# An encoder block on 8 cores: key order, bf16 gate weights, earlier constants, and five moved pieces of work

## The chip, the cores and the metric

The kernel runs on all 8 cores of one Trainium2 chip. Each core runs the same program on its own half of one batch element's sequence (4 batches, 2 halves); there is no traffic between cores. The metric is the device time of the slowest core in microseconds (us). On a core, TensorE (PE in the tables) multiplies, VectorE (DVE), ScalarE (ACT) and GpSimd (POOL) work on its results, and SyncE (SP) does nothing but issue transfers and wait. Each engine takes its instructions in the order in which they were written.

## The reference

The block is one layer of a bidirectional encoder, with D_MODEL 2048, 4096 positions, 6 differential heads of 128 (values 256 wide), a Fourier branch 512 wide and a feed-forward width of 5632.

```python
h = rmsnorm(x, g_mix); z = h @ w_in            # q | k | v | fourier | gate_a | gate_f
q = partial_rope(q, cos, sin); k = partial_rope(k, cos, sin)
p = softmax(q k^T / sqrt(128))                 # two maps per head
o = (p[0] - lam * p[1]) @ v
o = rmsnorm(o, g_subln) * (1 - LAMBDA_INIT)
branch_a = o @ w_attn_branch
branch_f = real(fft2(f, axes=(positions, channels), norm="ortho")) @ w_four_branch
x = x + (sigmoid(gate_a) * branch_a + sigmoid(gate_f) * branch_f) @ w_out
h2 = rmsnorm(x, g_ffn)
x = x + (silu(h2 @ w_gate) * (h2 @ w_up)) @ w_down
out = rmsnorm(x, g_final)
```

## The kernel before, in words

Everything is written through a small recording layer. `mm`, `act`, `tt`, `ts`, `stt`, `cp` and `dma` append one instruction to one engine's list, and the layer adds the waits between engines from the tiles that an instruction reads and writes. Nothing is reordered: what is written first on an engine stands first in its queue. Activations are kept transposed (features on the 128 partitions, 512 tokens wide), so that products are `128x512` matmuls. SP issues nearly all loads and stores; POOL issues the weight loads, which convert float32 in HBM to bf16 on the way.

**Projection, passes 0 to 3 (0 to 1147 us).** A pass P holds 1024 tokens. Its work is a list `plan` of units `('u', P, m)`, each a pair m of 128-wide column blocks of `w_in`, done with seven products in place of eight (a Strassen-like form: `prod`, with sums of weights from `combine_b` on DVE), and one entry `('f', P, None)` for the Fourier columns. Passes 0 and 1 are the core's own tokens and do all columns (gates only in pass 0; the other half of the gates is done inside the attention); passes 2 and 3 are the other half's tokens, and need only keys and values: 12 units each, in the orders `o2_m` and `o3_m` over `oth_m`. There `oth_m[0:6]` are the value pairs, `oth_m[6:9]` key pairs without rotation, and `oth_m[9:12]` key pairs that get rotary embedding (`rope`, six more DVE and three more ACT instructions a unit). While a pass runs, `form_gen` prepares the next pass's tokens in small steps between the products: loads of xT, squares on ACT with sums on DVE, then, in the last third, scaling and the operand sums on DVE. PE has 8 banks of PSUM for this, a unit uses 4. Results leave through 4 output buffers (`outb`) and SP. In pass 3 SP also loads the tables and data of the Fourier stage (`d_pre`, `d_load_tab`, `d_load_f`).

**Fourier stage (1147 to 1227 us).** 8 groups `gi` of 32 matmuls `ps<-d_t,d_f`, combined on DVE and ACT into `d_x`, and finished by `d_out(gi)`, which writes `yT_scr`. Constants of the attention (ones, lambda, the gains) are made at the head of this stage.

**Attention (1227 to 2281 us).** 24 steps `si` = (head h, query block qb of 512), each of 32 steps G (`r = G % 32`). A step G is: two score matmuls of 128 queries with 1024 keys (`rec_S`), one ACT exponential over `128x1024` (`rec_exp`), and beside them some value matmuls of the step si-1 (`pv_gen`) and some gate matmuls (`gate_gen`). A query tile `it` of 128 takes 8 steps G: 4 for the first map (into `p1b[it % 3]`), 4 for the second (into `p2b[it % 2]`). After that, `later` runs `combine_p` (DVE: scale both maps, add) and `turn` (SP: a transposing DMA of half a tile into `aT`). The keys of head h, map c, lie in `kT[(2*h + c) % 3]` and are loaded by `c_load_k`, the values by `c_load_v` (transposing DMAs too). `epilogue` does the head norm: `e1` is a ones matmul in one of two banks `pg`, which it shares with the gates, `e2` is on ACT, `e3` on DVE. The gates take 32 weight tiles (`gw_issue`), which are the columns that pass 0 had already loaded and converted once.

**Output projection and feed-forward (2281 to 4502 us).** The branches are joined, multiplied with `w_o`, and the sums of squares for the norm are reduced over partitions by a ones matmul (`make_R`) and turned into scales on ACT (`fin_R`), in `Rb`. Then come two halves `hf` of 1024 tokens: 44 gate/up blocks, then 16 blocks `dc` of the down projection, each for two token blocks j of 512. At the end 32 DVE instructions scale the output tiles and SP stores them.

## Time and profile before

| | |
|---|---|
| median of 3 runs | 4502.16 us (4494.06 to 4900.55) |
| the profiled execution | 4503.35 us, its slowest core (core 3) 4501.8 us from first to last instruction |
| cores | 4474.6 to 4501.8 us, granted TensorE clock 0.973 to 0.974 |
| PE, DVE, ACT busy | 4161.6 us (92%), 2600.3 us (58%), 1474.9 us (33%) |
| POOL busy | 270.8 us (6%) |
| DMA | 658.66 MB, 146 GB/s on average |

The busy share of PE is what is near its limit. A profiled execution lies 1.55 us above its own slowest core's span and 1.2 us above the median, so times below are changes to 4503.35. A row of a timeline reads: start, duration, engine, line and operation, the tile written, the tiles read, the shape, how many in a row, and in brackets the idle time just before with what ended it. `PEclk` is the granted share of TensorE's clock, DMA share the mean busy share of the 16 DMA engines.

### The profile page before, as it was taken

The numbers are of one execution on the slowest core, as the hardware profiler recorded it, in microseconds if no ns is written. First come the engines' busy times: TensorE is split into PE (matmuls) and PEld (weight loads), VectorE is DVE, ScalarE is ACT, GpSimd is POOL, SyncE is SP. The second block draws the span as 40 slices with busy tenths as digits, with TensorE's granted clock in tenths as the row PEclk, the third lists the DMA queues.
The fourth block names the chain that finished last, engine by engine and source line by source line (L and its number), as shares of the span: only waits on it lengthen the run. The fifth ranks groups of instructions, "written<-read, shape, count | busy, mean of one in ns | idle before, by whom it ended". The sixth has DMA issues, their size and how long they took to land.

```text
span 4501.8 us, 57298 instructions; the slowest of 8 cores (4474.6 to 4501.8 us)
## 1 busy us (share of the span) xinstructions
PE 4161.6 (92%) x18808; PEld 1844.2 (41%) x18808; DVE 2600.3 (58%) x3940; ACT 1474.9 (33%) x2583; POOL 270.8 (6%) x516
## 2 busy tenths in 40 slices
PE   6898999988898899879889997999999999999997
PEld 2443443433343334333334443444444444444443
DVE  6586667665266666656646445666642257776112
ACT  2322232312288888868821121111110011111000
POOL 0000000000000000000000000000000000000000
PEclk9999999999999999989999998999999999999998
DMA  6875686847598899998975697555557766665454
GB/s 161 200 157 124 129 190 134 185 102 179 139 186 152 164 171 168 167 150 151 167 196 156 170 236 201 85 86 91 87 114 160 158 128 132 127 134 93 92 103 128
DMA packets 678754, 658.66 MB, mean 146 GB/s; under 512 B 474944, under 2 KB 515904, under 8 KB 676416
## 3 DMA queue, kind: packets, MB, share of 16 engines
q0 software_dynamic: 73728, 264.27, 35.8%
q1 hardware_dynamic: 604736, 390.72, 35.4%
q8 instruction: 158, 2.59, 0.2%
q14 instruction: 132, 1.08, 0.1%
HBM read 692.61 MB, written 113.25 MB: 179 GB/s over the span
## 4 chain that ended last, share of the span: by engine, by line
PE 72%; DVE 8%; DMA 7%; SPq 5%; issue 4%; ACT 3%; DVEq 0%; ACTq 0%
PE ps L279 72%; SPq L954 3%; SPq L314 2%; DMA b_h<-xT 2%; ACT c_p L290 2%; DVE b_t L293 1%; DMA c_a<-c_p 1%; DVE c_p L297 1%; DVE b_h L302 1%; DMA c_k<-k_scr 1%; SPq L905 1%; DMA x_scr<-te 1%; DVE b_c L293 1%; ACT b_t L290 1%; DVE c_p L293 1%
## 5 line engine op out<-in xcount | busy, mean ns | idle before, releaser
L290 ACT ACTIVATE c_p<-ps 128x1024 bf16<-128x1024 f32 x768 | 783.1, 1022 | 193.6 <-PE ps L279 129.5
L279 PE MATMUL ps<-f_h,wc 128*128 128x512 bf16 x3520 | 775.1, 379 | 0.0
L279 PE MATMUL ps<-g_a,wr 128*128 128x512 bf16 x2816 | 608.1, 379 | 0.0
L279 PE MATMUL ps<-b_h,b_c 128*128 128x512 bf16 x2272 | 524.2, 388 | 87.7 <-ACT b_t L290 67.2
L279 PE MATMUL ps<-c_k,c_q 128*128 128x512 bf16 x1536 | 471.4, 389 | 84.8 <-ACT c_p L290 53.8
L279 PEld LDWEIGHTS ps<-f_h,wc 128*128 128x128 bf16 x3520 | 344.6, 98 | 416.5 <-issue 2.2
L279 PE MATMUL ps<-c_a,c_v 128*128 128x512 bf16 x1536 | 456.8, 389 | 5.1 <-DMA c_a<-c_p 4.5
L279 PEld LDWEIGHTS ps<-g_a,wr 128*128 128x128 bf16 x2816 | 275.6, 98 | 332.2
L293 DVE TENSOR_TENSOR gr<-ps,gr 128x512 f32<-128x512 f32 x352 | 242.3, 689 | 278.6 <-PE ps L279 278.5
L279 PEld LDWEIGHTS ps<-b_h,b_c 128*128 128x128 bf16 x2272 | 223.0, 100 | 380.6 <-issue 134.3
L279 PE MATMUL ps<-c_h,c_w 128*128 128x512 bf16 x1024 | 344.9, 388 | 35.4 <-DVE c_z L308 21.6
L279 PE MATMUL ps<-f_h,wr 128*128 128x512 bf16 x1408 | 320.6, 381 | 6.3 <-DVE f_h L293 6.2
L293 DVE TENSOR_TENSOR b_t<-ps,b_t 128x512 f32<-128x512 f32 x247 | 168.7, 687 | 216.8 <-PE ps L279 106.1
L297 DVE TENSOR_SCALAR c_p<-c_p,c_r 128x2048 bf16<-128x2048 bf16 x384 | 271.1, 748 | 11.2 <-DVE c_r L297 1.4
L279 PEld LDWEIGHTS ps<-c_k,c_q 128*128 128x128 bf16 x1536 | 145.1, 99 | 290.0 <-issue 152.6
L279 PE MATMUL ps<-b_h,b_w 128*128 128x512 bf16 x1136 | 256.8, 379 | 0.0
L293 DVE TENSOR_TENSOR c_p<-c_p,c_p 128x2048 bf16<-128x2048 bf16 x192 | 235.2, 1225 | 20.3 <-DVE c_p L297 0.5
L279 PEld LDWEIGHTS ps<-c_a,c_v 128*128 128x128 bf16 x1536 | 153.4, 100 | 200.7 <-issue 32.2
L279 PE MATMUL ps<-e_m,wr 128*128 128x512 bf16 x1024 | 221.3, 379 | 0.0
L279 PEld LDWEIGHTS ps<-f_h,wr 128*128 128x128 bf16 x1408 | 138.2, 98 | 175.1 <-issue 10.9
L290 ACT ACTIVATE b_t<-ps 128x512 f32<-128x512 f32 (+1 forms) x107 | 63.5, 594 | 400.1 <-PE ps L279 316.6
L279 PE MATMUL ps<-e_on,wr 128*128 128x512 bf16 x768 | 177.9, 382 | 10.6 <-DMA e_on<-oT_scr 5.9
(119 smaller groups left out, 3850.8 us busy)
## 6 DMA issues: line engine op xcount, KB each, us to landing
wr<-w_gu POOLq DMA_DIRECT2D x176, 512.0 KB, 6.9
b_w<-w_z POOLq DMA_DIRECT2D x144, 512.0 KB, 9.2
b_h<-xT SPq DMA_DIRECT2D x64, 512.0 KB, 15.9
wr<-w_dn POOLq DMA_DIRECT2D x64, 512.0 KB, 5.9
tm<-x_scr SPq DMA_DIRECT2D x96, 256.0 KB, 4.9
c_w<-w_z POOLq DMA_DIRECT2D x32, 512.0 KB, 7.6
z_scr<-c_z SPq DMA_DIRECT2D x64, 256.0 KB, 3.4
ez<-z_scr SPq DMA_DIRECT2D x32, 512.0 KB, 7.8
```

The source lines that it names most:

```text
L279: S.op('pe', lambda e: e.matmul(o, lhsT=l, rhs=r, start=st, stop=sp, skip_group_check=cont), reads, writes)
L290: S.op('act', lambda e: e.activation(out=o, in_=i, func=func, scale=scale, **kw), reads, writes)
L293: S.op(eng, lambda e: e.tensor_tensor(out=o, in0=a, in1=b, op=op), reads, writes)
L297: S.op(eng, lambda e: e.tensor_scalar(out=o, in0=a, scalar1=s1, scalar2=None, op0=op0), reads, writes)
L302: S.op(eng, lambda e: e.scalar_tensor_tensor(out=o, in0=a, scalar=s, in1=b, op0=op0, op1=op1), reads, writes)
L314: S.dma(q, lambda e: e.dma_start(out=o, in_=i), reads, writes, sem)
L905: S.dma('sp', lambda e: e.dma_start_transpose(out=vb[:, 8 * j:8 * j + 8, :], in_=vT_scr[2 * h:2 * h + 2, :, j * 1024:(j + 1) * 1024].rearr ...
L954: S.dma('sp', lambda e, A=A, P1=P1, sl=sl, hf=hf, qt=qt: e.dma_start_transpose(out=A[:, 16 * hf:16 * hf + 16, qt * 128:(qt + 1) * 128], in ...
```

## The change

Eight edits: (1) the order `o2_m` of pass 2; (2) in pass 0, each gate unit's converted weights are stored to a new scratch tensor `wb_scr` by SP, and `gw_issue` later loads from there; (3) the attention's constants are made at the program's start; (4) the Fourier tables are loaded in pieces of four k blocks, two pieces a unit from the third unit of pass 3, and all before the stage but the last table; (5) in the attention, `gmap` gives another order of query tiles and maps in the first half of a head's first query block and in the second half of its last, and key and value loads are moved; (6) the head norm's `e1` takes the bank that no gate matmul is using, when the gate's k stands between 5 and 10, and does not advance the rotation of the two banks; (7) `make_R` and `fin_R` of token blocks 2 and 3 move from ahead of the feed-forward to its third block; the last Fourier group's `d_out` moves into the attention; (8) the last two blocks dc of the down projection run by token block, and 12 of the 32 output tiles are scaled and stored beside the last product.

```diff
+            if P == 0 and m[0] >= 36:
+                gp = (m[0] - 36) // 2
+                dma('sp', wb_scr[gp], cur[0][:].rearrange("p (u a) k n -> p u (a k) n", u=2), [cur[1]], [d_wb[gp]], f'fo0_{gp}')
...
-                dma('pool', wg[i % 3][:], w_z[36 + i], [], [t_wg[i % 3]], f'wr{i % 3}')
+                dma('pool', wg[i % 3][:], wb_scr[i // 2, :, i % 2], [d_wb[i // 2]], [t_wg[i % 3]], f'wr{i % 3}')
...
-        o2_m = oth_m[0:6] + oth_m[7:12] + oth_m[6:7]
+        o2_m = oth_m[7:8] + oth_m[9:12] + oth_m[0:6] + oth_m[8:9] + oth_m[6:7]
...
+        def gmap(G):
+            si, r = G // 32, G % 32
+            b, ch = r // 4, r % 4
+            qt, c = b // 2, b % 2
+            if (si % 4 == 0 and r < 16) or (si % 4 == 3 and r >= 16):
+                qt, c = (b // 4) * 2 + b % 2, (b // 2) % 2
+            return si, r, qt, c, ch
...
             def e1():
-                st['p'] = pgget()[0:2]
+                if gst['k'] is not None and not 5 <= gst['k'] <= 10:
+                    later(1, e1)
+                    return
+                j_ = pgi[0] % 2
+                flush_pg(j_)
+                st['p'] = (pg[j_], t_pg[j_])
                 PB, tpb = st['p']
+                later(2, e2)
+                later(5, e3)
...
-            later(7, e1)
-            later(9, e2)
-            later(12, e3)
+            later(5, e1)
...
-        c_load_k(1, 0)
-        for j in range(4):
-            c_load_v(0, j)
...
+            if G == 2:
+                d_out(7, bk[4:6], t_bk[4:6], 'dve')
...
+            if G in (13, 18, 21, 26):
+                c_load_v(0, (13, 18, 21, 26).index(G))
             if r == 1:
-                if qb == 1 and 0 < h and h + 1 < NH:
+                if qb == 1 and h + 1 < NH:
                     c_load_k(h + 1, 0)
...
-            if qb == 3 and r == 27 and h + 1 < NH:
+            if qb == 3 and r == 23 and h + 1 < NH:
                 c_load_k(h + 1, 1)
...
-    for q in range(2, 4):
-        pb = bank()
-        make_R(q, pb)
-        fin_R(q, pb)
...
+            if hf == 0 and ff == 2:
+                for q in range(2, 4):
+                    pb = bank()
+                    make_R(q, pb)
+                    fin_R(q, pb)
...
+            dn_out(14, 0, dn_mm(14, 0))
+            dn_out(15, 0, dn_mm(15, 0))
+            pb = dn_mm(14, 1)
+            dn_R(0)
+            dn_out(14, 1, pb)
+            pb = dn_mm(15, 1)
+            for dc in range(12):
+                dn_fin(dc, 0)
+            dn_out(15, 1, pb)
+            dn_R(1)
+            for dc in range(12, 16):
+                dn_fin(dc, 0)
+            for dc in range(16):
+                dn_fin(dc, 1)
```

**SyncE at the start of pass 3, before** (`d_t` are the Fourier tables, `d_f` the Fourier data, `b_o` the four output buffers, numbers are the built program's own):

```order
171 L314 DMA f_scr<-b_o_53 128x2x512
172 L314 DMA f_scr<-b_o_54 128x2x512
173 L314 DMA d_t_74<-dft_c 128x8x512 x2
174 L314 DMA d_t_75<-dft_s 128x8x512 x2
175 L314 DMA d_f<-f_scr 128x8x512
176 L314 DMA k_scr<-b_o_55 128x1024
177 L314 DMA k_scr<-b_o_56 128x1024
178 L314 DMA k_scr<-b_o_53 128x1024
179 L314 DMA k_scr<-b_o_54 128x1024
```

**The same place of the change:**

```order
190 L315 DMA f_scr<-b_o_61 128x2x512
191 L315 DMA f_scr<-b_o_62 128x2x512
192 L315 DMA d_t_82<-dft_c 128x4x512 x2
193 L315 DMA k_scr<-b_o_63 128x1024
194 L315 DMA k_scr<-b_o_64 128x1024
195 L315 DMA d_t_82<-dft_c 128x4x512 x2
196 L315 DMA k_scr<-b_o_61 128x1024
197 L315 DMA k_scr<-b_o_62 128x1024
198 L315 DMA d_f<-f_scr 128x8x512 x2
```

Five large loads stood ahead of the key stores of two units; now two half-sized pieces stand ahead of each unit's two stores.

**ScalarE across the end of the first head, before** (second half of its last query block, first half of the next head's first; `c_p_109` to `111` are `p1b`, `112` and `113` are `p2b`):

```order
523 L290 ACTIVATE c_p_113,c_l_100<-ps 128x1024 x4
524 L290 ACTIVATE c_p_110,c_l_99<-ps 128x1024 x4
525 L290 ACTIVATE c_p_112,c_l_99<-ps 128x1024 x4
526 L290 ACTIVATE c_p_111,c_l_100<-ps 128x1024 x4
527 L290 ACTIVATE c_p_113,c_l_100<-ps 128x1024 x4
```

**The same place of the change** (`c_p_111` to `113` are `p1b` here, `114` and `115` are `p2b`):

```order
515 L291 ACTIVATE c_p_113,c_l_107<-ps 128x1024 x4
516 L291 ACTIVATE c_p_111,c_l_108<-ps 128x1024 x4
517 L291 ACTIVATE c_p_114,c_l_107<-ps 128x1024
518 L291 ACTIVATE c_rstd<-ps,c_eps 128x512
519 L291 ACTIVATE c_rstd<-c_rstd 128x512
520 L291 ACTIVATE c_p_114,c_l_107<-ps 128x1024 x3
521 L291 ACTIVATE c_p_115,c_l_108<-ps 128x1024 x4
522 L291 ACTIVATE c_p_112,c_l_107<-ps 128x1024 x4
523 L291 ACTIVATE c_p_113,c_l_108<-ps 128x1024 x4
524 L291 ACTIVATE c_p_114,c_l_107<-ps 128x1024 x4
525 L291 ACTIVATE c_p_115,c_l_108<-ps 128x1024 x4
```

Maps came in the order first, second, first, second; around the head's end they now come first, first, second, second. The second map's keys are first used 8 steps into the head, not 4, and the first map's last use is 8 steps before its end, not 4. `c_p_113`, filled from r = 16, is complete with its second map at r = 27 and filled again from r = 4 of the next head.

**VectorE at the program's end, before** (`h_x` the output tiles, `xl` and `tm` the residual tiles and squares):

```order
3753 L293 TENSOR_TENSOR h_x_161<-ps,tm_151 128x512
3754 L293 TENSOR_TENSOR k_R<-k_R,tm_153 128x512
3755 L293 TENSOR_TENSOR h_x_161<-ps,tm_152 128x512
3756 L293 TENSOR_TENSOR k_R<-k_R,tm_154 128x512
3757 L302 SCALAR_TENSOR_TENSOR h_x_161<-h_x_161,k_gfin,k_R 128x512 x32
```

**The same place of the change:**

```order
3757 L294 TENSOR_TENSOR h_x_163<-ps,xl_184 128x512
3758 L294 TENSOR_TENSOR k_R<-k_R,tm_155 128x512
3759 L303 SCALAR_TENSOR_TENSOR h_x_163<-h_x_163,k_gfin,k_R 128x512 x12
3760 L294 TENSOR_TENSOR h_x_163<-ps,xl_186 128x512
3761 L294 TENSOR_TENSOR k_R<-k_R,tm_156 128x512
3762 L303 SCALAR_TENSOR_TENSOR h_x_163<-h_x_163,k_gfin,k_R 128x512 x20
```

Twelve of the 32 scalings now stand ahead of the last block's sum.

## Rows read from the trace of the kernel before

**Rows 1.** Busy us of each engine by stretch; then clock, DMA share, GB/s
```profile
770.00:969.00 199.00, 171.75 (x743) 74.26 (x741) 140.03 (x194) 55.85 (x97) 13.79 (x26) 0.93 0.67 151
969.00:1147.00 178.00, 165.69 (x748) 73.64 (x746) 91.97 (x124) 37.53 (x64) 13.18 (x25) 0.96 0.74 167
1227.00:2281.00 1054.00, 928.93 (x4071) 397.15 (x4071) 676.03 (x1041) 848.92 (x1580) 18.63 (x35) 0.95 0.93 163
```

**Rows 2.** TensorE, passes 0 to 2: timeline; waits of 695 to 765 us
```profile
374.85 3.52 PE L279 MATMUL ps<-b_h,b_c 128*128 128x512 bf16 x15 [1.45 <-ACT b_t L290]
PE ps L279 <- DVE b_t L293: 10.3, 6, 3.8
853.98 8.75 PE L279 MATMUL ps<-b_h,b_c 128*128 128x512 bf16 x32 [3.42 <-ACT b_t L290]
941.13 6.31 PE L279 MATMUL ps<-b_h,b_c 128*128 128x512 bf16 x16 [8.87 <-ACT b_t L290]
```

**Rows 3.** Timeline of SyncE and TensorE, start of pass 3
```profile
1002.65 21.70 SPq L314 DMA_DIRECT2D d_t<-dft_s  x2
1050.84 2.72 PE L279 MATMUL ps<-b_h,b_c 128*128 128x512 bf16 x6 [10.12 <-ACT b_t L290]
```

**Rows 4.** Timeline, Fourier stage and first scores
```profile
1159.26 0.29 DVE L293 TENSOR_TENSOR c_z<-c_z 128x128 f32<-128x128 f32 x1 [7.51 <-DMA c_z<-lams]
1163.17 6.14 PE L279 MATMUL ps<-d_t,d_f 128*128 128x512 bf16 x16 [7.93 <-DVE d_x L293]
1227.38 1.01 PE L279 MATMUL ps<-c_k,c_q 128*128 128x512 bf16 x2 [5.96 <-ACT c_p L290]
```

**Rows 5.** Waits of TensorE, 1227 to 2300 us (total us, times, longest us)
```profile
PE ps L279 <- ACT c_p L290: 53.8, 32, 10.9
PE ps L279 <- DMA c_k<-k_scr: 30.1, 5, 11.7
PE ps L279 <- DVE c_z L308: 21.6, 9, 3.1
PE ps L279 <- DVE c_z L297: 9.3, 8, 2.2
```

**Rows 6.** Busy us, clock, DMA share and GB/s, after a key wait
```profile
1403.00:1408.00 5.00, 4.95 (x14) 1.84 (x15) 0.00 (x0) 2.23 (x4) 0.00 (x0) 0.58 0.52 117
```

**Rows 7.** Timeline around the key wait at 1917 us
```profile
1910.92 2.83 SPq L314 DMA_DIRECT2D c_k<-k_scr  x4
1929.19 1.01 PE L279 MATMUL ps<-c_k,c_q 128*128 128x512 bf16 x2 [11.70 <-DMA c_k<-k_scr]
```

**Rows 8.** Attention: ScalarE's waits, queue q0, and transposes' landing
```profile
ACT c_p L290 <- DMA c_a<-c_p: 41.8, 10, 12.1
q0 software_dynamic: 5040, 18.35, 11.8%
DMA to landing us min/median/max: 4.3/4.9/18.4
```

**Rows 9.** Page part 5: scaling and adding of the probabilities on VectorE
```profile
L297 DVE TENSOR_SCALAR c_p<-c_p,c_r 128x2048 bf16<-128x2048 bf16 x384 | 271.1, 748 | 11.2 <-DVE c_r L297 1.4
L293 DVE TENSOR_TENSOR c_p<-c_p,c_p 128x2048 bf16<-128x2048 bf16 x192 | 235.2, 1225 | 20.3 <-DVE c_p L297 0.5
```

**Rows 10.** Stretch of pass 0, and queue q1 over 116 to 330 us
```profile
167.00:217.00 50.00, 50.00 (x234) 22.69 (x232) 36.55 (x52) 20.29 (x38) 4.23 (x8) 1.00 1.02 222
q1 hardware_dynamic: 14416, 20.19, 29.7%
```

**Rows 11.** Timeline of TensorE, end of the output projection
```profile
2779.28 3.94 PE L1289 MATMUL ps<-k_R,k_ones 128*128 128x512 f32 x4 [22.46 <-DVE k_R L293]
2790.61 1.01 PE L279 MATMUL ps<-f_h,wr 128*128 128x512 bf16 x2 [5.60 <-DVE f_h L293]
```

**Rows 12.** Timeline, end of the program
```profile
4467.74 1.02 PE L1289 MATMUL ps<-k_R,k_ones 128*128 128x512 f32 x2
4472.60 21.29 DVE L302 SCALAR_TENSOR_TENSOR h_x<-h_x,k_gfin,k_R 128x512 f32<-128x512 f32 x32 [2.31 <-ACT k_R L290]
```

More of the change, by code:

```diff
@@ L741, in build_nc @@
                 d_pre()
-            if P == 3 and m == o3_m[4]:
-                d_load_f(1)
-            if P == 3 and m == o3_m[5]:
-                d_tab1c()
+            if P == 3 and m in o3_m[2:]:
+                for f_ in d_q[0:2]:
+                    f_()
+                del d_q[0:2]
             B1, B2, B3, B4 = [pzget() for _ in range(4)]
@@ L1084, in build_nc @@
         rec_S(0)
-        d_out(7)
         hg_load(1, 3)
@@ L1490, in build_nc @@
                 w_issue()
-        for j in range(2):
-            pb = bank()
-            make_R(hf * 2 + j, pb)
-            fin_R(hf * 2 + j, pb)
         if hf == 0:
+            for j in range(2):
+                dn_R(j)
             fin_q = [(dc, j) for j in range(2) for dc in range(16)]
-    for j in range(2):
-        for dc in range(16):
-            x3, t3 = x3T[:, dc, j * 512:(j + 1) * 512], t_x3[dc][j]
-            stt('dve', x3, x3, g_fin_s[:, dc:dc + 1], Rb[:, 2 + j, :], ALU.mult, ALU.mult, [t3, t_cst, t_R[2 + j]], [t3])
-            d = S.tile("out"); d_outt.append(d)
-            dma('sp', out[dc, :, (2 + j) * 512:(3 + j) * 512], x3, [t3], [d], f"fo{j}_{dc}")
+        else:
+            xl2 = Ring("xl", 176 * K1, 4, [128, 512], F32, 2 * K1)
+            dn_load(14)
+            dn_load(15)
+            dn_out(14, 0, dn_mm(14, 0))
[12 more added lines that the diff above has]
+                dn_fin(dc, 1)
     S.finish('sp', d_outt)
```

163 lines of the change are left out of this document (96 added, 67 removed).

## The prediction

> **What bounds the kernel now.** I read the stretches first, then TensorE's waits by releaser, then the timeline at each long wait. PE is busy 92% of the span, so what can be won is its idle time and what the clock loses behind it. The stretch table shows where that lies: pass 2, pass 3 and the attention are at a granted clock of 0.93, 0.96 and 0.95 and have idle PE [rows 1]. In the attention 1054 us are 768 steps G, 1.37 us a step, with PE busy 929 us and the DMA engines at 0.93. ScalarE has 849 us of it. So PE is the bound with short stalls, each of which costs its own length and some clock, and DMA is nearly full beside it. No wait of the program is long for one reason; the change takes away a number of them. I go through them in the order of time, counting idle time plus lost clock.
>
> **Start.** Three more SP issues stand ahead of the first loads of xT; at 0.7 us each (four take 2.83 us [rows 7]) that is +2 us. ScalarE's new exponential waits for a 256 KB load that lands before xT's first tile does. Bounds 0 and +5.
>
> **Copies in pass 0: +5.** 16 stores of 1 MB are added on SP's queue q1. That queue moved 20.19 MB in 29.7% of 214 us, 318 GB/s [rows 10], so they are 53 us of all 16 engines, in a stretch where the share already is 1.02 for 50 us [rows 10] while PE was busy in all of them. The first copy stands ahead of pass 1's first xT load, on which PE waits: +3.3 us (1.05 MB at 318 GB/s). The others lie beside PE work, and a weight buffer is now free only once its copy has landed; loads of weights are issued about two units ahead, some 24 us at the pace of the stretch (56 products a unit, 234 in 50 us [rows 10]) of use. If that cover goes, the 53 us less the free 18% of the engines (39 us) come through, 14 us. I take +5, with bounds 0 and +20.
>
> **Order of pass 2: -17.** The stretch of pass 2 holds 199 us with 27.2 us of idle PE (199 less 171.75) and 0.07 x 199 = 13.9 us of lost clock [rows 1], 41 in all. The waits lie where the rotary units meet the DVE-heavy last third of `form_gen`; the longest is 8.87 us on ScalarE [rows 2], which itself waits for DVE. Pass 1 shows that last third beside value units: 10.3 us of DVE waits in 70 us [rows 2] and about 1.4 us of clock. The new order leaves this (11.7), the wait of 3.42 for xT with its clock (5), and three rotary units, of which each costs 1.45 even without a `form_gen` [rows 2], with clock 1.75: 5.2. Together 22, so -19. Rotary units now share DVE with the sums of squares, which is nearly full for three units, so I take -17 (bounds -25 and +5).
>
> **Fourier tables in pieces: -14.** SP was held 21.70 us by two loads [rows 3], key stores came behind them, the four output buffers filled, DVE and then ScalarE stood, and PE 10.12 us [rows 3]. The stretch has 12.3 us of idle and 0.04 x 178 = 7.1 of lost clock [rows 1]; three rotary units keep 5.2 of these 19.4. Two pieces a unit pass in half the time of one table and the output buffers hold for a unit. Bounds -19 and 0. The Trainium skill says in "DMA: Bandwidth & Descriptors" (section Bandwidth) that transfers should be batched to 1 MiB or more for 75% of peak, which speaks against halving them to 512 KB; no row here has the same load in both sizes. Read so, the 6.3 MB of pieces would take about a third more of nearly full engines, some 10 us, of which half might reach PE; this term would be -9 and the sum 4401.
>
> **Constants early, last Fourier group later: -18.6.** DVE waited for the lambdas and did its sum only at 1159 us, PE stood 7.93 us [rows 4], and at the usual half clock for the next 6 us another 2.7 is lost (after a key wait 5 us have 0.58 [rows 6]): -10.6. What is late next is nothing that the trace shows: tables 0 are loaded by then. The first exponentials waited for ScalarE, which waited for the stores of the last groups: 5.96 us [rows 4] and 3 of clock; the last group now goes through DVE in two idle banks: -8. Bounds -22 and -5.
>
> **Attention: -55.9, the term that decides.**
> Keys: 30.1 us in 5 waits [rows 5], and four of them long enough to leave 5 us at clock 0.58 (2.1 each) [rows 6]: 38.5. The worst load is issued at 1910.92 and PE goes on at 1929.19 [rows 7], so 18.3 us from issue to use. It had some 5 steps; now it is issued at r = 23 and first used 17 steps later, 23 us at 1.37. All five go.
> Gates: waits of a gate matmul for DVE's copy, 21.6 + 9.3 = 30.9 us in 17 times [rows 5]. They come about once for each of the 23 epilogues, because the ones matmul takes one bank out of the rotation and the next gate falls back into the bank just left. With the other bank and no turn of the rotation they go; the clock behind them I put at 0.5 us each, a quarter of what a key wait leaves, for most are half a key wait or shorter and stay without it: 8.5, together 39.4.
> New in their place: `p1b` is filled again sooner. Before, 15 steps lay between a tile's `turn` and the reuse; at 11 places (six heads' beginnings, five ends) there are 7, that is 9.6 us. Queued behind a late `turn` is ScalarE's exponential, and PE's next score waits for that. The turn needs DVE's two scalings and one add, 2 x 0.75 + 1.2 = 2.7 us [rows 9], and 4.9 us to land, at worst 18.4 [rows 8]. The median makes 7.6, the worst 21.1, so a place costs between 0 and 11.5 us. ScalarE already waits 41.8 us in 10 times for such landings [rows 8], with 11 to 15 steps in hand. I take 10 us for the 11 places, near the median. The epilogue's PE and the sums `lac`, needed again after 3 steps and not 7: +4 (bounds 0 and 15).
> Gate weights from `wb_scr`: queue q0 took 11.8% of 1063 us for 35 loads [rows 8], 3.6 us each; at q1's rate 1.65. 32 loads save at most 62 us of DMA, at least 0. The DMA work of the stretch (0.93 x 1054 = 980 us) would then be as dense in the shorter stretch as now, so the 41.8 us stay; I count 0 (bounds -20 and +10).
> When PE stalls less, the next engine is nearer: I give back a tenth of 77.9, +8. Sum: -77.9 + 10 + 4 + 8 = -55.9, bounds -100 and +40. The 53.8 us of PE behind ScalarE [rows 5] otherwise stay.
>
> **Partition sum later: +1.7.** PE's wait of 22.46 us stands in the list ahead of `make_R`, but 7 matmuls after that it waits 5.60 more for `f_h` and goes on at 2790.61 [rows 11]. That operand comes from DVE, whose queue the edit doesn't touch. So the idle time moves and keeps its end; what is moved costs two float32 sums on a PE that is full, about 1 us for two at full clock, and two table loads on ScalarE. Bounds 0 and +4.
>
> **The end: -10.4.** DVE begins 32 scalings at 4472.60 and takes 21.29 us [rows 12]; 8.4 MB at 318 GB/s is 26.4 us, so stores set the end, at 4501.8, 33.9 us after PE's last product, behind which the first ones matmul stands at 4467.74 [rows 12]. Now the first 12 run beside the last product. After it come DVE's sum and square, the ones matmul, two ScalarE steps (about 6 us, as before plus the rest of the 12), and then 16 tiles: 13.2 us of stores and 2.5 to land, 22.5 in all, plus 1 for the earlier `make_R` inside PE's list. Bounds -14 and -6.
>
> **Sum.** 2 + 5 - 17 - 14 - 18.6 - 55.9 + 1.7 - 10.4 = -107.2, and 4503.35 - 107.2 = 4396 us. More than half of the span (2791 to 4468 us) isn't touched. The median of the runs stands 1.2 us lower than the profiled execution, which I leave out.
>
> **Rivals.**
> *Attention stays full of DMA.* For it: share 0.93, 41.8 us of ScalarE behind transposes. Key and gate waits go, but transposes land later in a denser stretch and stall at other steps: the term shrinks to -15, 4437 us. Against it: the long key waits end on SP's order, not on bandwidth. Chance 0.28.
> *Relief adds up.* The gate loads at q1's rate free 62 us of DMA, the 41.8 us halve with their share of the 53.8, and nothing is given back: attention -95, 4357 us. Chance 0.15.
> *Reused probabilities become the bound (slower).* At 11 places a turn lands as the worst does now, 11.5 us late each: 127 us in place of 10, 4396 + 117 = 4513 us. It decides from a landing of about 17.5 us after issue at each place (10.6 us late). Against it: the median is 4.9, and no key load stands next to those turns any more. Chance 0.03.
> *Copies stall pass 0.* Share over 1.0 for 200 us, weights late: +20 in place of +5, 4411 us. Chance 0.09.
> The forecast has 0.45.
>
> **How the numbers follow.** 90 us, 2%, is about what a measurement of this kernel tells from no change: faster by more means under 4412. That is the forecast nearly whole (0.39 of its 0.45), the relief (0.15), half of the copies case (0.05) and a little of the first rival (0.02): 0.61. Slower by over 2% would need more than the slower rival's middle gives, 0.02. Same has 0.37. The range takes the first rival in and the relief case with a margin: 4347 to 4458; above it lie the slower rival and a small part of the first, below it a part of the relief case.
>
> **What would show it.** In the profile of the changed kernel: pass 2 about 180 us long with no wait over 5; no SP issue over 10 us at the start of pass 3; no 8 us wait at the Fourier stage; no wait on `c_k`; `c_z` waits near 0; ScalarE's waits for `c_a` near 42 us, and if they are 80 or more the first rival is right; the wait ahead of the feed-forward still ending about 34 us after the last product of `w_o`; the end about 23 us after PE's last product. The prediction is wrong above all if the attention is not between 970 and 1020 us long.

## The result and the profile after

The changed kernel takes 4424.43 us (median of 4 runs, 4421.19 to 4692.14); the ratio to the kernel before is 0.983 with a 95% interval of 0.981 to 0.985, so it is 66 to 86 us faster. The forecast was 4396, the range 4347 to 4458: the direction and the range held, and the gain between the profiled executions came out at 78 us instead of 107. The case that the forecast thought likeliest did not come: it gave 0.61 to a gain of over 2%, and 1.7% [1.5%, 1.9%] is the case to which it gave 0.37. The profiled execution took 4425.17 us; its slowest core (core 7) spans 4423.3 us, the quickest 4381.9, at granted clocks of 0.978 to 0.983 (0.973 to 0.974 before).

To see where the time went I took, on each core, the start of the first product of each stage, and the median of the cores. A pass is taken from its Fourier columns (the entry `'f'` of the plan, one unit into the pass), because these products are easy to find in a trace. In some executions the cores of one die run at a lower granted clock; they are left out of every ratio (4692.14 here), e13 has none for that reason, and in the profiled executions of e6, e8, e12 and e13 only the other die's four cores are read. The columns are: up to the Fourier columns of pass 2, from there to those of pass 3, to the first product of the Fourier stage, to the first score of the attention, to its last score, to the last product of all, and to the end (us).

```
kernel                  passes 0-1  pass 2  pass 3  Fourier  attention  rest     end    in all
before                    787.2     200.1   166.6    71.8     1043.3    2189.1   33.4   4491.6
after                     808.0     190.3   153.5    61.9      976.3    2187.6   25.6   4403.2
e1_no_copies              791.8     186.5   153.4    62.4      998.4    2193.2   26.0   4411.7
e2_copies_unused          812.6     187.3   153.3    63.3     1002.0    2193.8   25.0   4437.2
e3_late_copies            800.2     187.7   154.5    63.1      987.5    2193.0   25.7   4411.7
e4_old_map_order          808.8     189.8   153.0    61.9      991.0    2190.0   25.6   4420.1
e5_old_norm_bank          816.7     187.1   155.9    62.6     1004.6    2192.3   24.5   4443.8
e6_old_pass2_order        816.0     199.9   153.7    62.6      989.3    2200.2   25.9   4447.6
e7_one_burst              817.6     186.9   177.7    61.7      976.4    2195.8   25.4   4441.6
e8_sum_ahead_of_ff        815.2     188.1   153.4    62.5      984.1    2193.8   26.3   4423.4
e9_copies_act_queue       822.7     186.3   152.2    61.7      977.9    2188.7   26.3   4415.7
e10_1mb_pieces            817.0     188.7   152.2    62.6      973.4    2193.4   25.6   4412.8
e12_every_other           790.3     188.3   152.8    61.9      986.4    2191.5   25.6   4396.9
e13_other_half            798.7     188.4   153.3    62.4     1000.1    2194.5   25.9   4423.3
```

The rows also show what this table can't resolve. Kernels that are alike in passes 0 and 1 differ there by chip: 808 to 813 us (after, e2, e4), and 815 to 818 on the chip of e5 to e10. Those alike in the attention take 973 to 978 us where all eight cores are read (after, e7, e9, e10), but 984 and 989 where four are (e8, e6). So a comparison is good to some 5 us on one chip by all eight cores, and to some 10 to 15 otherwise; in the short stages it is 1 or 2.

Where a length alone misleads, two more readings are given as means of the cores: TensorE's idle time in the stage, and the lost clock, which is the length of the stage times one less its mean granted clock. In the attention they are 122 and 44 us before, and 72.0 and 23.0 after.

The stretches of the changed kernel's slowest core, passes 2 and 3 cut at the same places as in [rows 1]: pass 2 with its first unit, pass 3, the Fourier stage, the attention.

```profile
801.00:993.00 192.00, 170.20 (x742) 73.88 (x741) 139.41 (x194) 56.84 (x97) 13.71 (x26) 0.95 0.74 158
993.00:1159.00 166.00, 161.22 (x738) 71.99 (x737) 91.03 (x123) 36.41 (x62) 13.18 (x25) 0.99 0.77 178
1159.00:1220.00 61.00, 61.00 (x284) 27.70 (x283) 20.25 (x32) 16.59 (x31) 0.00 (x0) 1.00 0.62 164
1220.00:2209.00 989.00, 912.80 (x4054) 392.53 (x4052) 666.12 (x1029) 846.07 (x1579) 19.74 (x35) 0.97 0.90 173
```

Pass 2 keeps 21.8 us of idle PE (27.2 before) at a clock of 0.95 (0.93). Pass 3 and the Fourier stage are at a clock of 0.99 and 1.00 and have 4.8 us of idle PE and none. The attention is 989 us long on this core (976 by the medians) at a DMA share of 0.90 (0.93 before) and a clock of 0.97 (0.95). Its waits, against [rows 5] and [rows 8] (total, times, longest), TensorE first:

```profile
PE ps L280 <- ACT c_p L291: 56.9, 40, 9.9
PE ps L280 <- DMA c_a<-c_p: 10.5, 3, 4.4
PE ps L280 <- DVE c_sq L294: 7.1, 1, 7.1
PE ps L280 <- DVE c_r L949: 6.2, 3, 2.1
ACT c_p L291 <- DMA c_a<-c_p: 46.2, 18, 10.3
```

No wait on `c_k` and none on `c_z` is left in the list. ScalarE's waits for the transposes' landing are 46.2 us where they were 41.8 (by the mean of the cores 47 and 38). Queue q0 moved the same 5040 packets and 18.35 MB into SBUF in a smaller share of the engines (11.8% before [rows 8]), and the row below it is the landing of a half-megabyte gate load, which was 7.6 us from the float32 weights:

```profile
q0 software_dynamic: 5040, 18.35, 7.5%
c_w<-wb_scr POOLq DMA_DIRECT2D x29, 512.0 KB, 5.7
```

What the changed kernel pays for that stands in passes 0 and 1. In the timeline of TensorE a weight is late; between 64 and 780 us there was no such wait before:

```profile
228.35 1.87 PE L280 MATMUL ps<-b_h,b_w 128*128 128x512 bf16 x4 [7.10 <-DMA b_w<-w_z]
```

### The profile page after: what moved, and what is told of

The parts are those of the page before. It is cut to its first block, busy times and chain, and to the rows that moved or that the text cites. A ratio compares the mean times of both kernels' runs of the same rounds, so it can differ in the third digit from the quotient of the medians.

```text
span 4423.3 us, 57322 instructions; the slowest of 8 cores (4381.9 to 4423.3 us)
## 1 busy us (share of the span) xinstructions
PE 4148.6 (94%) x18808; PEld 1840.5 (42%) x18808; DVE 2602.1 (59%) x3945; ACT 1475.3 (33%) x2583; POOL 272.8 (6%) x518
## 4 chain that ended last, share of the span: by engine, by line
PE 71%; DMA 9%; DVE 8%; issue 4%; SPq 4%; ACT 3%; DVEq 0%; ACTq 0%; POOL 0%; POOLq 0%
PE ps L280 71%; ACT c_p L291 2%; DMA c_a<-c_p 2%; DMA wb_scr<-b_w 2%; DVE b_t L294 2%; SPq L968 2%; DMA b_w<-w_z 1%; DMA b_h<-xT 1%; SPq L912 1%; DVE c_p L298 1%; DVE b_h L303 1%; DVE b_c L294 1%; SPq L315 1%; DMA x_scr<-te 1%; ACT b_t L291 1%
## 5 line engine op out<-in xcount | busy, mean ns | idle before, releaser
L298 DVE TENSOR_SCALAR c_p<-c_p,c_r 128x2048 bf16<-128x2048 bf16 x384 | 271.1, 748 | 10.6 <-DVE c_r L298 0.5
L291 ACT ACTIVATE tm<-ps 128x512 f32<-128x512 f32 x88 | 52.5, 597 | 391.8 <-PE ps L280 391.8
## 6 DMA issues: line engine op xcount, KB each, us to landing
b_w<-w_z POOLq DMA_DIRECT2D x146, 512.0 KB, 10.4
wb_scr<-b_w SPq DMA_DIRECT2D x16, 1024.0 KB, 18.1
```

Source lines behind the costliest of these rows:

```text
L291: S.op('act', lambda e: e.activation(out=o, in_=i, func=func, scale=scale, **kw), reads, writes)
L298: S.op(eng, lambda e: e.tensor_scalar(out=o, in0=a, scalar1=s1, scalar2=None, op0=op0), reads, writes)
```

## The experiments

Each is the changed kernel with one edit. Ratios are to the kernel before on the same chip; for the changed kernel itself it was 0.983 [0.981, 0.985]. One thousandth is 4.5 us.

**No copies (e1).** Computes the same; the attention's gate weights come from the float32 weights again.

```
-            if P == 0 and m[0] >= 36:
+            if False:
-                dma('pool', wg[i % 3][:], wb_scr[i // 2, :, i % 2], ...
+                dma('pool', wg[i % 3][:], w_z[36 + i], ...
```

> The changed kernel without its copies of gate weights: pass 0 stores none, and the attention loads its 32 weight tiles from the float32 input again. Theory 1, the copies cost more than they give: passes 0 and 1, which were 18 us longer in the median of the cores, are as long as before (Fourier stage reached about 20 us sooner than in the changed kernel), the attention is 0 to 8 us longer, and the time is 4402 to 4412 us. Theory 2, the lighter gate loads are what made the attention shorter: its stretch grows by 20 us or more, and the time is 4420 us or more.

Measured: 0.984 [0.982, 0.986]. Each theory was right on one stage. In all the copies make next to no difference, and the table says why: without them passes 0 and 1 are 16 us shorter (791.8 against 808.0) and the attention 22 us longer (998.4 against 976.3). Two rows of the costliest groups between 144 and 535 us of core 7 show the price, the first two of the changed kernel:

```profile
L315 POOL DMA_DIRECT2D b_w<-w_z x52 | 27.4, 532 | 343.5 <-DMA wb_scr<-b_w 169.8 <-DVE b_t L294 84.2 <-PE ps L280 56.6
L294 DVE TENSOR_TENSOR b_s<-b_w 128x1024 bf16<-128x1024 bf16 x26 | 17.8, 684 | 37.5 <-DMA b_w<-w_z 37.5
```

and the same two without copies:

```profile
L315 POOL DMA_DIRECT2D b_w<-w_z x58 | 30.6, 531 | 355.0 <-PE ps L280 194.4 <-DVE b_t L294 116.7 <-DVE b_c L294 32.8
L294 DVE TENSOR_TENSOR b_s<-b_w 128x1024 bf16<-128x1024 bf16 x26 | 17.7, 682 | 1.1 <-DMA b_w<-w_z 1.1
```

POOL's weight loads wait for a copy to land (170 us in total; a copy takes a median of 18.1 us from issue to landing), DVE then waits 37.5 us for weights, and PE for both: from 64 us to the start of pass 2 it waits 72 us on core 7, and 52 without copies. A copy can also only be issued once its weights have landed, and SP, whose queue it stands in, waits 20.4 us in 5 times for that, with the loads and stores behind it. The stretches from 144 to 267 and to 400 us stand at DMA shares of 0.94 and 0.98 with the copies:

```profile
144.00:267.00 123.00, 113.35 (x513) 50.18 (x512) 71.12 (x101) 41.44 (x72) 8.98 (x18) 0.97 0.94 225
267.00:400.00 133.00, 120.08 (x537) 52.59 (x536) 100.40 (x136) 33.77 (x56) 11.05 (x21) 0.97 0.98 220
```

and without them at

```profile
144.00:267.00 123.00, 123.00 (x568) 55.74 (x567) 82.06 (x115) 45.15 (x79) 11.59 (x22) 1.00 0.84 179
267.00:400.00 133.00, 123.97 (x567) 54.36 (x566) 106.82 (x147) 34.16 (x58) 10.54 (x20) 1.00 0.74 158
```

The gain stands in the attention's waits without copies:

```profile
ACT c_p L291 <- DMA c_a<-c_p: 70.2, 30, 8.8
PE ps L280 <- ACT c_p L291: 74.6, 51, 8.3
```

and in q0's share there:

```profile
q0 software_dynamic: 5040, 18.35, 12.3%
```

ScalarE waits 70 us for transposes instead of 46, by the mean of the cores 63 instead of 47, and PE behind ScalarE 72 instead of 56. In all, PE is idle 90 us of the attention instead of 72 and the lost clock is 29 us instead of 23.

**Copies made but not used (e2).** The stores stay, the gate weights come from float32.

```
-                dma('pool', wg[i % 3][:], wb_scr[i // 2, :, i % 2], ...
+                dma('pool', wg[i % 3][:], w_z[36 + i], ...
```

> The 16 copies are stored in pass 0, but the attention loads its gate weights from the float32 input. Both theories expect passes 0 to 3 as in the changed kernel. Theory 1 (loads from the copies give little): 4424 to 4432 us. Theory 2 (they give 20 us or more): 4445 us or more. The attention's length should be that of the kernel with no copies at all, within 5 us.

Measured: 0.989 [0.985, 0.992], some 24 us slower than the changed kernel, and the attention 1002.0 us, 26 longer and within 4 of e1's, as expected. The time is near the second theory's 4445 us or more (4440.1 and 4452.9). Together with e1 this shows both halves apart: the copies cost 21 us (e2 against e1, on one chip; 16 if the changed kernel is set against e1), and their use brings 22 to 26.

**Only the last eight copies (e3).** Half of the gate weights are copied, those of the last eight units of the gates.

```
-            if P == 0 and m[0] >= 36:
+            if P == 0 and m[0] >= 52:
```

> Only the last 8 of the 16 gate units of pass 0 store copies, when the next pass's xT loads are done; the first 16 weight tiles of the attention come from the float32 input. If the copies cost by standing in the way of xT loads while the DMA engines are full, two thirds or more of the 18 us in passes 0 and 1 go: 4406 to 4414 us. If each copy costs the same by holding its weight buffer, half of it goes: 4414 to 4420 us.

Measured: 0.983 [0.979, 0.986], the changed kernel's. Half of the price goes (800.2 us) and half of the relief too (987.5), as for copies that each cost the same.

**The old order of maps and keys (e4).** The second map's keys are loaded at r == 27 again, and the steps of a head's first and last block run in the old order.

```
-            if (si % 4 == 0 and r < 16) or (si % 4 == 3 and r >= 16):
+            if False:
-            if qb == 3 and r == 23 and h + 1 < NH:
+            if qb == 3 and r == 27 and h + 1 < NH:
```

> The changed kernel with the old order of query tiles and maps everywhere, and the second map's keys loaded at step 27 again. Theory: the five waits for keys are back, 30 us idle and 8 of clock, less what the sooner reuse of the probability buffers now costs (about 10): 4424 + 28 = 4452 us, attention about 28 us longer, waits on c_k of 20 to 35 us. Rival: the new order only traded key waits for waits on transposes, so the time stays within 8 us of 4424, with fewer waits on c_a.

Measured: 0.985 [0.983, 0.987], the attention 14.7 us longer (991.0), between the theory's 28 and the rival's 8. TensorE's and ScalarE's waits there:

```profile
PE ps L280 <- ACT c_p L291: 49.9, 33, 18.1
PE ps L280 <- DMA c_k<-k_scr: 23.1, 5, 6.5
PE ps L280 <- DVE c_r L949: 13.7, 7, 2.2
ACT c_p L291 <- DMA c_a<-c_p: 37.2, 11, 18.4
```

The five key waits are back with 23.1 us. But ScalarE's waits for transposes went the other way: a mean of 26 us over all cores, in 11 times, where the changed kernel has 47 in 18, and PE's waits behind ScalarE fell from 56 to 40. The new order takes 23 us of key waits away, and 6 at `c_r` (13.4 against 7.7 by the mean), and gives 17 back at the reused probabilities. PE's idle time in the attention is 8 us less by it (72.0 against 80.1) and the lost clock 4 us less.

**The head norm in the next bank of the rotation (e5).**

```
-                j_ = pgi[0] % 2
-                flush_pg(j_)
-                st['p'] = (pg[j_], t_pg[j_])
-                later(2, e2)
-                later(5, e3)
+                st['p'] = pgget()[0:2]
...
-            later(5, e1)
+            later(7, e1)
+            later(9, e2)
+            later(12, e3)
```

> The changed kernel with the head norm as before: the ones matmul takes the next bank of the gates' rotation and turns it, and its three steps come 7, 9 and 12 steps behind the products with v. Theory 1, the term as I priced it: the rotation is broken once for each of the 23 epilogues, so some 17 waits of a gate matmul for DVE's copy come back, 31 us with 8 of lost clock, and the attention is 39 us longer (about 4463 us in all). Theory 2, which the run with the old map order suggests: a wait of PE that is taken away there only lets PE run into ScalarE or a transpose a little later, so that of 39 us about a third counts: the waits for DVE's copy come back in the list of waits, but those for ScalarE shrink by more than half as much, and the attention is 10 to 18 us longer (4434 to 4442).

Measured: 0.989 [0.985, 0.992]; the attention is 1004.6 us, 28 longer than the changed kernel's and 15 to 31 longer than that of the five others on this chip (e6 to e10). The waits for DVE's copy are back as they were [rows 5]:

```profile
PE ps L280 <- ACT c_p L291: 61.4, 39, 17.4
PE ps L280 <- DVE c_z L309: 19.4, 9, 3.1
PE ps L280 <- DVE c_z L298: 14.4, 8, 4.0
PE ps L280 <- DVE c_r L949: 2.7, 2, 1.7
```

Here little stands in for them: by the mean of the cores 33 us of `c_z` come back, while the changed kernel has 3 us more than this one at ScalarE, and 7.7 us at `c_r`, where its ones matmul waits (4.6 in the kernel before). PE's idle time is 23 us more (94.8 against 72.0) and the lost clock 4.5 us more (27.5 against 23.0), which together are the longer stage. That is the first theory in its waits and between both in what it costs.

**The old order of pass 2 (e6).**

```
-        o2_m = oth_m[7:8] + oth_m[9:12] + oth_m[0:6] + oth_m[8:9] + oth_m[6:7]
+        o2_m = oth_m[0:6] + oth_m[7:12] + oth_m[6:7]
```

> The changed kernel with pass 2's units in the old order. Theory 1, my term: pass 2 is 17 us longer, with PE waits on ScalarE and DVE of 8 to 9 us again, 4441 us in all. Theory 2: the rotary units' waits are only moved to where they meet the sums of squares, as the changed kernel's own waits of 5.63, 3.78 and 3.32 us in pass 2 suggest; pass 2 is then 6 to 10 us longer, 4431 to 4435 us in all.

Measured: 0.986 [0.983, 0.988], and pass 2 is 199.9 us, as in the kernel before (200.1), against 190.3: 10 us, the size of the second theory. TensorE's waits between 816 and 1016 us:

```profile
PE ps L280 <- ACT b_t L291: 23.6, 4, 9.0
PE ps L280 <- DVE b_t L294: 4.4, 3, 3.3
```

and in the changed kernel between 808 and 998:

```profile
PE ps L280 <- ACT b_t L291: 12.5, 4, 5.6
PE ps L280 <- DVE b_t L294: 9.3, 6, 3.8
```

The new order halves the waits behind ScalarE and doubles those behind DVE. In the timeline of the changed kernel's core 7 the first sort is at the rotary units (three of 5.63, 2.10 and 2.22 us, where ScalarE itself waits for DVE), and 8.3 of the 9.3 us behind DVE are at the value units beside the last third of the norm.

**The Fourier tables in one burst (e7).** The same pieces of 512 KB, all in one unit.

```
-                for f_ in d_q[0:2]:
+                for f_ in d_q:
                     f_()
-                del d_q[0:2]
+                del d_q[:]
```

> The changed kernel with all twelve pieces of the Fourier tables and the two loads of f issued in one unit of pass 3, instead of two a unit; the pieces keep their 512 KB. Theory 1: spacing is what counts, SP is held by them, key stores come behind, the output buffers fill and PE stands: pass 3 is 10 to 15 us longer. Theory 2: what held SP before was the size of one table's load, so the burst in pieces costs under 3 us. Theory 3, the full engines are what counts, and then it is longer still in the unit of the burst but given back in the units after: under 5 us in all.

Measured: 0.988 [0.985, 0.991], and pass 3 is 177.7 us instead of 153.5, 11 more even than in the kernel before. SP's and TensorE's timeline:

```profile
1021.31 23.52 SPq L315 DMA_DIRECT2D d_t<-dft_c  x4
1045.03 8.37 SPq L315 DMA_DIRECT2D d_f<-f_scr  x2
1053.45 14.30 SPq L315 DMA_DIRECT2D d_t<-dft_s  x4
1067.85 9.27 SPq L315 DMA_DIRECT2D d_t<-dft_c  x4
1090.25 5.11 PE L280 MATMUL ps<-b_h,b_c 128*128 128x512 bf16 x13 [21.96 <-ACT b_t L291]
```

SP is held for 56 us. The first two pieces still pass in 1.4 us; the third and the fourth take 22.0, as long as the two whole loads of [rows 3]. Key stores come out behind the burst, and PE stands 21.96 us. In the changed kernel the six pairs of pass 3, spaced by a unit, take 1.1 to 4.2 us each, one of them:

```profile
1069.25 1.41 SPq L315 DMA_DIRECT2D d_t<-dft_s  x2
```

**Pieces of 1 MB, one a unit (e10).** The same bytes of tables a unit in half as many pieces; the two loads of f, 1 MB each, now go one a unit as well.

```
-                for k0 in range(0, 16, 4):
-                    d_q.append(lambda rb=rb, w=w, k0=k0: d_load_tab(rb, w, k0, 4))
+                for k0 in range(0, 16, 8):
+                    d_q.append(lambda rb=rb, w=w, k0=k0: d_load_tab(rb, w, k0, 8))
...
-                for f_ in d_q[0:2]:
+                for f_ in d_q[0:1]:
```

> The changed kernel with the Fourier tables loaded in pieces of 1 MB, one a unit, instead of 512 KB, two a unit: the same bytes in a unit. Theory 1: what counts is that not more than about 1 MB stands ahead of a unit's stores, so nothing changes: passes 2 and 3 and the Fourier stage within 2 us of the changed kernel's. Theory 2, from the Trainium skill (DMA: Bandwidth & Descriptors, section Bandwidth), that transfers should be 1 MiB or more: the pieces of 512 KB cost about a third more of the engines for 6 MB, and 1 MB ones make pass 3 some 5 us shorter.

Measured: 0.984 [0.978, 0.990]; pass 3 is 152.2 us, the changed kernel's within 1.3 us, and SP issues a piece in

```profile
1087.73 0.43 SPq L315 DMA_DIRECT2D d_t<-dft_s  x1
```

So spacing is the effect, and the size of a piece has none that shows. The rule that I weighed in the forecast (the Trainium skill, "DMA: Bandwidth & Descriptors", section Bandwidth: batch to 1 MiB or more) would by my estimate have made these pieces 5 us better than the small ones (-14 against -9 in my sum). For this stage the runs don't bear that out: 1.3 us is what shows, within what the table resolves, and that with a DMA share of 1.02 while the small pieces ran (1020 to 1104 us of core 7).

**The partition sum ahead of the feed-forward (e8).**

```
     h_form(0, 7)
+    for q in range(2, 4):
+        pb = bank()
+        make_R(q, pb)
+        fin_R(q, pb)
```

(and not behind the feed-forward's third step).

> The changed kernel with the two partition sums of the second half of the tokens back ahead of the feed-forward. Theory 1, my term: the idle time between the last product of w_o and the feed-forward keeps its end, set by DVE's f_h, so putting the sums back makes the kernel 1 to 2 us faster or the same. Theory 2, which the changed kernel's profile suggests (28 us from the last product of w_o to the resumed feed-forward instead of 34): the operand f_h waited for the sum after all, and it is 4 to 6 us slower.

Measured: 0.983 [0.980, 0.986], no difference. TensorE's timeline of the changed kernel from the last product of `w_o` on:

```profile
2679.70 12.25 PE L280 MATMUL ps<-e_m,wr 128*128 128x512 bf16 x56
...
2699.11 0.58 PE L280 MATMUL ps<-f_h,wr 128*128 128x512 bf16 x1 [6.07 <-DVE f_h L294]
2712.68 0.58 PE L280 MATMUL ps<-f_h,wr 128*128 128x512 bf16 x1 [13.00 <-DVE f_h L294]
2719.70 4.00 PE L280 MATMUL ps<-f_h,wr 128*128 128x512 bf16 x9 [6.43 <-DVE f_h L294]
```

and with the sums put back:

```profile
2711.99 4.21 PE L1316 MATMUL ps<-k_R,k_ones 128*128 128x512 f32 x4 [22.81 <-DVE k_R L294]
...
2723.66 4.00 PE L280 MATMUL ps<-f_h,wr 128*128 128x512 bf16 x9 [4.98 <-DVE f_h L294]
```

25.5 us idle in three pieces here, 27.8 in two there, and both end at DVE's `f_h`. From the last product of `w_o` to the resumed feed-forward it is 29 to 35 us on the cores before, 28 to 39 after: the idle time has moved and kept its end.

**The copies on ScalarE's queue (e9).**

```
-                dma('sp', wb_scr[gp], ...
+                dma('act', wb_scr[gp], ...
```

> The changed kernel with its 16 stores of bf16 gate weights issued by ScalarE on a queue of their own instead of by SP. Theory 1: the 18 us that the copies cost in passes 0 and 1 come from the weight buffer that each copy holds until it has landed (POOL's issues of weight loads wait 170 us for the copies' landing between 144 and 535 us). The engines are as full as before, but a copy no longer stands behind the xT loads in SP's queue, so it lands in under 12 us instead of 18, and half or more of the 18 us comes back: 4408 to 4416 us. Theory 2: the stretch is simply full (share 0.94 to 0.98), the time goes to 16.8 MB more of traffic whichever queue carries it, and the kernel stays within 4 us of the changed one. A third way: ScalarE's own work stands behind the issues (each waits for the weights to land and be free), and the passes get longer still.

Measured: 0.984 [0.982, 0.987], and passes 0 and 1 are 822.7 us, 6 more than e10's on the same chip. The passes got longer, as the third way said, but its reason isn't seen: the sixteen issues take ScalarE 0.33 us each, and in its timeline no work that was ready stands behind one. The first theory's cause did go, as the copies' landing and POOL's row between 144 and 535 us show:

```profile
wb_scr<-b_w ACTq DMA_DIRECT2D x16, 1024.0 KB, 12.3
```

```profile
L315 POOL DMA_DIRECT2D b_w<-w_z x50 | 26.4, 532 | 354.5 <-PE ps L280 150.2 <-DVE b_t L294 112.4 <-DMA wb_scr<-b_w 47.8
```

POOL waits 48 us for copies instead of 170 and PE has 1.2 us of late weights instead of 8.0. Yet PE's waits from 64 to 535 us are longer in other places (35.6 and 13.9 us in the changed kernel):

```profile
PE ps L280 <- ACT b_t L291: 39.1, 11, 13.6
PE ps L280 <- DVE b_t L294: 18.2, 7, 13.9
ACT b_o L788 <- DMA ga_scr<-b_o: 28.3, 6, 7.9
```

ScalarE now waits 19.8 us for xT (4.3 in the changed kernel) and 28.3 us for gate stores (0.3), and the longest of PE's waits, 13.9 us, stands behind SP, which four stores of `hT_scr` hold for 24.2 us. So the held buffer isn't the whole price: the 16 copies are paid on either queue, with later loads and stores of others in this nearly full stretch. That the added bytes do it is argued from this, not shown.

**Every other pair copied (e12).**

```
-            if P == 0 and m[0] >= 36:
+            if P == 0 and m[0] >= 36 and m[0] % 4 == 2:
```

(and the gate loads take the copy where there is one).

> The changed kernel with only every other pair of gate tiles stored as bf16 (8 stores, 8.4 MB in place of 16.8); the other 16 gate tiles of the attention are loaded from the float32 weights. Theory 1: the cost is a buffer held too long, and with a free buffer between two copies it is mostly absorbed: passes 0 and 1 cost 0 to 5 us over the kernel without copies, half of the relief of some 22 us in the attention stays, and the kernel ends 3 to 6 us ahead of the changed one. Theory 2: price and relief both go by bytes, as in the run with the late copies only: +9 and -11, and nothing changes in all.

Measured: 0.980 [0.977, 0.982]. Its best two executions took 4409.64 and 4409.90 us, the best of e10 on the same chip 4421.15; the interval still touches the changed kernel's. Passes 0 and 1 take 790.3 us, 27 less than in e10 and no more than without copies, and the attention 986.4. PE's idle time and lost clock from 60 us to the end of passes 0 and 1 say the same: 54.7 and 15.4 us, 55.9 and 15.4 without copies, 68.4 and 23.0 in the changed kernel. That is at least half of the relief for no price, which neither bytes nor e3 (8 us for as many copies) would give. Nor is it the free buffer that the first theory names: POOL still waits 61.0 us for copies to land, more than e9's 48. ScalarE's wait for transposes there:

```profile
ACT c_p L291 <- DMA c_a<-c_p: 50.5, 21, 10.7
```

**The other half (e13).**

```
-... m[0] % 4 == 2:
+... m[0] % 4 == 0:
```

> As the run with every other pair stored, but with the other eight pairs: those with an even number, the first of them the copy that stands ahead of pass 1's first xT load in SP's queue. Theory 1: what made every other pair cheap is the free weight buffer between two copies, so this half is as cheap: passes 0 and 1 within 3 us of that run, 0 to 5 us over the kernel without copies, the attention within its scatter of some 6 us, and the kernel 8 to 15 us ahead of the changed one (4406 to 4416 us; ratio to the kernel before 0.979 to 0.982). Theory 2: the choice of pairs decides. The first copy delays xT by the 3.3 us that I priced, and the start of pass 0's norm with it, so that passes 0 and 1 are 4 to 8 us longer than in that run and nothing is left of the gain.

Measured: on die 0 the slowest core took a median of 4433.2 us against 4506.2 of the kernel before, a ratio of 0.984, near the changed kernel's and 8 to 22 us short of the first theory's 0.979 to 0.982. Passes 0 and 1 (798.7) lie 8 us above e12 and 9 under the changed kernel, as the second theory said; the cause that it named, a delayed xT, is not shown. The attention's 1000 us are no sign of a missing relief: PE is idle 77 us there, as in e12 (78) and in e8 and e6 (77 and 80, all copies), against 90 without copies; the stage is long by its lost clock, 44 us where these have 24 to 27. What differs from e12 in the early stage is SP's wait for weights ahead of a copy: 4.2 to 7.9 us on the four cores here, 0.8 or none in e12, 14 to 23 in the changed kernel and in e10. It fits the price of these three, but not e3's or e9's, which have a price and no such wait. So e12's gain is not confirmed as one of spacing.

## Why the prediction was right, and where its terms were off

By the medians of the cores the change is worth 88.4 us, and by the slowest core 78.5. The forecast's 107.2, term by term:

| term | forecast | measured | from |
|---|---|---|---|
| start | +2 | +2.1 | start of the ones matmul of pass 0's norm |
| copies in passes 0 and 1 | +5 | +19 | 808.0 - 787.2 - 2.1; e1: +16 |
| order of pass 2 | -17 | -9.8 | table; e6: -9.6 |
| Fourier tables | -14 | -13.1 | table |
| constants early | -10.6 | -9.9 | table |
| attention, last Fourier group with it | -63.9 | -67.0 | table |
| partition sum | +1.7 | -1.5 with all from there to the last product | table; e8: none |
| end | -10.4 | -7.8 | 25.6 - 33.4; core by core -9.3 |

**The step that failed is the price of the copies.** "The others lie beside PE work", and 14 us if the cover goes: I took +5 and let the cover hold. It didn't. The loads were issued two units ahead, but a copy lands 18.1 us after its issue and holds the buffer until the load behind it is late, and e9 shows that with the buffer free earlier the copies cost as much all the same. The measured 16 to 21 us is at the upper bound of 20 that I had drawn. The rival that named it (0.09) was right on this term.

**The relief was counted at nothing and is worth 22 to 26 us,** beyond the bound of 20. The argument was that DMA work would be as dense in the shorter stretch as now. It is not: q0 fell from 11.8% to 7.5%, which is 49 us less of the engines (11.8% of 1063 is 125, 7.5% of 1020 is 77), the share from 0.93 to 0.90, and ScalarE's waits for transposes are 47 us and not e1's 63. What I predicted of these waits ("near 42 us") came true for a reason that I had excluded. The first rival, an attention that stays full of DMA, had a sound core: without relief, e1's attention is 998.4 us, 45 less than before; the forecast had 64 and this rival 23, each with the 8 of the Fourier group.

**Keys and gates were over-priced, the reuse under-priced.** Keys with the reused probabilities: forecast -38.5 + 10, measured 14.7 (e4). The 23 us of key waits do go; but the waits at transposes that the shorter reuse brings are 20 us of ScalarE and 17 of PE, not 10, at the place that I had named. Gates with their epilogue: forecast -39.4 + 4, measured 28 (e5; 15 to 31 on its chip). The waits of 31 us were right to 3; of the 8.5 us of clock behind them 4.5 show, and 3 us come back at `c_r`. These two over-pricings and the missing relief offset each other, so that the term that decides was right to 3 us by its sum, not by its parts. That it was so near is luck.

**Pass 2** was priced at 17 and gave 10. The last third of the norm beside value units was priced right: 10.3 us of waits in the forecast, 8.3 measured. What was too cheap are the three rotary units beside the sums of squares: 1.45 us of waits each in the forecast and 2 us for sharing DVE, 10.9 us in all measured, with one wait of 5.63, which the forecast said would not be over 5. The stretch keeps 21.8 us of idle PE and 0.05 x 192 = 9.6 of lost clock, 31 us of the 41; the forecast left 24.

**The end** was right. Core by core, it is 34.0 us from PE's last product to the end before and 24.7 after, by the medians, so -9.3; the -7.8 of the table comes of medians of different cores. On core 7 the sixteen last scalings begin 8.5 us after PE's last product:

```profile
4389.70 9.44 PE L280 MATMUL ps<-g_a,wr 128*128 128x512 bf16 x43
4404.01 2.01 PE L1316 MATMUL ps<-k_R,k_ones 128*128 128x512 f32 x2 [4.87 <-DVE k_R L294]
4393.72 8.03 DVE L303 SCALAR_TENSOR_TENSOR h_x<-h_x,k_gfin,k_R 128x512 f32<-128x512 f32 x12
4403.78 2.73 DVE L303 SCALAR_TENSOR_TENSOR h_x<-h_x,k_gfin,k_R 128x512 f32<-128x512 f32 x4
4407.69 10.69 DVE L303 SCALAR_TENSOR_TENSOR h_x<-h_x,k_gfin,k_R 128x512 f32<-128x512 f32 x16 [1.17 <-ACT k_R L291]
```

Four of the first sixteen scalings stand behind the last sum in DVE's queue (2.73 us) and the sixteen end at 4418.4; the last stores land 4.9 us later.

**What remains** of the 29 us between forecast and result: copies 14, pass 2 7, the end 3 (core by core 1), the other terms -5 together, 19 by the medians; the other 10 are the slowest core. It stood 10.2 us over the median of the cores before and 20.1 after, and the metric is that core. Why the changed kernel's cores differ more stays open; at the Fourier columns of pass 2 its core 7 stood at 817.2 us, 34 behind core 3 of before, where the medians are 21 apart.

**The start** came out at 2.1 us, but not as told. The landing that the forecast took to be early enough was not: the first product of all begins at 24.5 us instead of 15.6, and 7 of these 9 us are made up before the sum of the norm, in a stretch where PE waits for its operands in any case (35 us of waits up to 64 us, before and after).

Still open: why every other pair costs nothing in e12 and the other eight pairs some 7 us in e13 on another chip, and so whether half the copies beat the changed kernel. The runs bear out that they are at least as good.

## What to carry to other kernels

A transfer moved to an earlier stage has two prices, one in each stage; read both shares before counting either as zero. Here sixteen stores of 1 MB in a stretch with a share of 0.74 to 0.84 cost nearly what they later saved, and half of them, with gaps, may cost nothing.

When a wait is removed by an earlier load that also shortens the time to a buffer's reuse, price both at once: here 23 us of key waits went and 17 us of waits behind transposes came. And when a queue is held by large loads, space them, here one megabyte a unit: it was worth 13 us, and the size of the pieces nothing that shows.

For a forecast on many cores, add the spread of the cores to the range of the sum: 10 us of an 88 us gain were lost to the slowest core alone.

## What was not expected of the hardware

A gate load of 524,288 bytes of bf16 in SBUF took 3.5 us of all 16 engines from float32 (12.3% of 998 us over 35 loads, in e1). In the changed kernel the same 35 loads take 7.5% of 1020 us, 76.5 us; six of them (`wr<-w_af`) still convert, which by estimate leaves 1.9 us for each of the 29 from bf16. I had put 1.65 us from q1's rate, and a saving of 62 us for 32 loads; by the same estimate it was some 50, and about half of it reached PE.

SP's issue time of the same instruction is no property of it: within one burst (e7) the first pair of 512 KB loads took SP 1.4 us and the second 22.0; a unit apart the same pairs took 1.1 to 4.2.

Passes 0 and 1 with all copies, the stage that is fullest of DMA, took 808 to 813 us in three executions and 815 to 818 in five on one other chip: some 6 us went with the chip and not with the kernel. In the attention the length hid what the waits showed: e13's 1000 us have the idle time of a kernel with copies (77 us) and a lost clock of 44 us, where e12, e8 and e6 have 24 to 27.
